# A decoder step whose GpSimd queue takes page numbers from an SBUF copy of the page table instead of DRAM

## The reference

```
page_table (DEC_BATCH, PAST_LEN // PAGE_SIZE) int32, logical page -> physical page
kidx_past = cache_kidx[page_table].reshape(b, past, IDX_DIM)
score     = sum over heads of relu(qi . kidx) * wi
_, idx    = lax.top_k(score, topk)
rows      = page_table[idx // PAGE_SIZE] * PAGE_SIZE + idx % PAGE_SIZE
k_sel, v_sel = k_pool[rows], v_pool[rows];  out = softmax(q . k_sel) @ v_sel
```

## Time and profile before

| what | value |
| --- | --- |
| median of three runs | 2094.11 us (2090.16 to 2096.39) |
| the profiled execution: span from the first to the last instruction | 2095.3 us; the page gives nothing outside it |
| PE busy | 1872.0 us, 89% |
| DVE, ACT, POOL busy | 55%, 42%, 9% |
| mean granted clock of TensorE | 0.913 of full speed |
| data moved | 365.41 MB, mean 174 GB/s |

### The profile page before, as it was taken

The page is one execution under the profiler, slowest core; times in us unless marked ns, Lnnn a source line. Parts: engine busy times, 40 slices in busy tenths (PEclk is TensorE's granted clock), DMA queues, the critical chain, the costliest instruction groups (busy, mean ns, idle before and its releaser), DMA issues.

```text
span 2095.3 us, 26096 instructions
## 1 busy us (share of the span) xinstructions
PE 1872.0 (89%) x9628; PEld 1571.3 (75%) x9628; DVE 1149.1 (55%) x1375; ACT 870.6 (42%) x987; POOL 190.7 (9%) x235
## 2 busy tenths in 40 slices
PE   6998669757998887899999989999999999997898
PEld 3998548645886666799799768867876886885798
DVE  4875335897851111122344337873885885885532
ACT  3332235445432222232132326753773773774432
POOL 1110112332321211100000000000000000000000
PEclk9999879878999887799999859997999999999999
DMA  7554213322445234347365517984995995996440
GB/s 209 133 137 115 71 51 94 88 62 79 131 142 138 89 103 132 94 127 258 123 179 144 153 41 274 366 285 145 367 366 162 364 371 188 333 366 204 141 126 26
DMA packets 389873, 365.41 MB, mean 174 GB/s; under 512 B 20804, under 2 KB 363892, under 8 KB 388664
## 3 DMA queue, kind: packets, MB, share of 16 engines
q1 hardware_dynamic: 381560, 345.03, 52.8%
q0 software_dynamic: 8192, 18.89, 3.0%
HBM read 353.15 MB, written 10.72 MB: 174 GB/s over the span
## 4 chain that ended last, share of the span: by engine, by line
PE 69%; DVE 10%; issue 9%; POOLq 9%; ACT 2%; DMA 1%; DVEq 0%; POOL 0%; SPq 0%; ACTq 0%
PE psum L1335 19%; PE psum L626 17%; POOLq L1183 8%; PE psum L643 8%; PE psum L699 5%; PE psum L1322 5%; PE psum L609 4%; PE psum L661 2%; PE psum L1263 2%; PE psum L575 1%; PE psum L692 1%; DVE arena L1980 1%; DVE arena L1978 1%; PE psum L1307 1%; ACT weights_high L1581 1%
## 5 line engine op out<-in xcount | busy, mean ns | idle before, releaser
L830 DVE TENSOR_TENSOR weights_low<-arena,weights_high 128x2048 fp32r<-128x2048 f32 x192 | 439.5, 2292 | 81.0 <-ACT weights_high L725 81.0
L1335 PE MATMUL psum<-input_high,weights_high 128*128 128x320 f32 x1264 | 414.9, 328 | 43.0 <-ACT arena L1644 23.8
L725 ACT ACTIVATE weights_high<-arena 128x2048 fp32r<-128x2048 f32 x192 | 367.3, 1916 | 90.6 <-PE psum L626 56.1
L1335 PE MATMUL psum<-input_low,weights_high 128*128 128x320 f32 x1264 | 403.8, 319 | 0.0
L1335 PE MATMUL psum<-input_high,weights_low 128*128 128x320 f32 x1264 | 403.3, 319 | 0.0
L1335 PEld LDWEIGHTS psum<-input_high,weights_high 128*128 128x128 f32 x1264 | 249.5, 197 | 59.7 <-ACT arena L1644 29.5
L1335 PEld LDWEIGHTS psum<-input_low,weights_high 128*128 128x128 f32 x1264 | 249.5, 197 | 1.2
L1335 PEld LDWEIGHTS psum<-input_high,weights_low 128*128 128x128 f32 x1264 | 248.5, 197 | 0.1
L1838 DVE TENSOR_TENSOR weights_low<-arena,weights_high 128x1024 fp32r<-128x1024 f32 x128 | 150.8, 1221 | 108.6 <-ACT weights_high L1581 108.5
L626 PE MATMUL psum<-weights_high,gathered_high 128*128 128x512 f32 x512 | 204.2, 399 | 0.0
L626 PE MATMUL psum<-weights_low,gathered_high 128*128 128x512 f32 x512 | 201.1, 393 | 0.0
(11 more groups left out here) (310 smaller groups left out, 2506.1 us busy)
## 6 DMA issues: line engine op xcount, KB each, us to landing
arena<-in_w SPq DMA_DIRECT2D x384, 512.0 KB, 7.5
arena<-in_w_in SPq DMA_DIRECT2D x64, 1024.0 KB, 5.7
arena<-in_w_out SPq DMA_DIRECT2D x16, 1024.0 KB, 5.9
arena<-in_w_ple_gate SPq DMA_DIRECT2D x16, 1024.0 KB, 6.9
arena<-in_cache_k POOLq DMA_DIRECT2D x64, 128.0 KB, 2.3
arena<-in_w_br_rnn SPq DMA_DIRECT2D x8, 1024.0 KB, 5.5
arena<-in_cache_v POOLq DMA_DIRECT2D x64, 128.0 KB, 2.3
arena<-in_w_br_attn SPq DMA_DIRECT2D x8, 1024.0 KB, 5.3
```

The costliest lines, as they stand in the source:

```text
L725: nc.scalar.activation(stage[m % STG][0][:], mslots[m % MRING], ACT.Identity).then_inc(s["high"], 1)
L830: v.tensor_tensor(lo[:], mslots[m % MRING], hi[:].bitcast(F32), ALU.subtract).then_inc(s["split"], 1)
L1335: last = mm(acc[0:m, 0:T], x[:, P * k:P * k + m], y[:], start=(k == 0 and n == 0), stop=(k == KD - 1 and n == 2))
```

## The change

The 64 table entries are copied by one DMA into a row of SBUF, `pages_i`, as POOL's first instruction. `page` then loads the register from there, and the queue waits for that copy once, ahead of the first page.

```
+        pages_i = nc.alloc_sbuf_tensor_at("pages_i", [1, NB * NPG], I32, offset=base + 4 * top[0])
+        take(NB * NPG)
...
+        pages_in = sem("pages_in")
...
         @block.gpsimd
         def _(pool):
+            pool.dma_start(pages_i[:], A["page_table"].rearrange("(o b) g -> o (b g)", o=1)).then_inc(pages_in, 16)
             nc.gpsimd.memset(wa[:], 0.0)
...
             def page(b, g):
-                return pool.value_load(A["page_table"][b:b + 1, g:g + 1], min_val=0, max_val=A["cache_k"].shape[1] - 1)
+                n = NPG * b + g
+                return pool.value_load(pages_i[0:1, n:n + 1], min_val=0, max_val=A["cache_k"].shape[1] - 1)
+
+            pool.wait_ge(pages_in, 16)
```

## The result

| | before | changed |
| --- | --- | --- |
| median (range, runs) | 2092.14 us (2084.86 to 2096.39, 4) | 1965.74 us (1964.02 to 1993.46, 4) |
| ratio, 95% interval | | 0.9435 [0.9381, 0.9488] |
| profiled execution, span | 2095.3 us | 1962.3 us (its time 1964.02) |
| mean granted clock | 0.913 | 0.952 |
| PE busy | 1872.0 us | 1815.9 us |

The change makes the kernel 126 us faster by the medians, 133.0 by the two spans. The forecast was 1981 us.

A forecast was written before the change was run, and what follows sets the result against it. POOL's issue of cache pages, not their bytes, was taken to bound index scores and sample attention. Gains of 35.9 + 79.9 = 115.8 us, less 3, gave 2095.3 - 113 = 1982, so 1981 us; range 1964 to 2020.

The forecast's parts named there:

- What bounds the kernel: Index scores and sample attention: PE waits 31.4 and 45.5 us for pages POOL issues late, then runs at low clock.
- A page's issue: POOL's queue: a page's 2.30 us falls to 1.4 with the number loaded from SBUF (1.17 to 1.42).
- The stalls: POOL's address loads of up to 3.54 us: gone if DRAM's; if the queue's, a page costs 1.65 us.
- Index scores: Both PE waits for pages of indexer keys go, with some slow clock: 35.9 us gained.
- Between the stages: From top-k to sample attention: everything shifts by the earlier gain, 0 us more, 5 us either way for DVE pieces.
- Sample attention: Six remaining passes run without waits at full clock, 173.0 us against 252.9: 79.9 us gained.
- The allowance: 3 us set against the gain because ACT and DVE get less time for the same steps.
- The sum: Whole kernel: 35.9 + 79.9 = 115.8 us, less 3; 2095.3 - 113 = 1982, so 1981.
- Low clock: Rival, sample attention: waits go but matmuls stay slow, only 77 us gained, 2017 us; chance 0.06.
- POOL binds: Rival, both stages: a page still costs 2.0 us, so some waits remain, 2018 us; chance 0.09.
- Slower: Rival, 128 pages: one SBUF load costs more than both DRAM loads; 2135 us at 2.0 us a load; chance 0.02.
- No change: Rival: PE waits at the same places for something later, such as softmax on DVE and ACT, 2094 us; chance 0.03.

The follow-up runs named there:

- e1: Changed kernel with only the indexer keys' pages numbered from SBUF, keys and values from DRAM as before; ratio 0.9797 to the kernel before, median 2058.13 us.
- e2: Changed kernel with only the keys' and values' pages numbered from SBUF, indexer keys from DRAM; ratio 0.9543 to the kernel before, median 1999.86 us.
- e6: Changed kernel without the two instructions that check a page number's bounds; ratio 0.94 to the kernel before, median 1966.27 us.
- e3: Changed kernel with each page number loaded from SBUF twice; ratio 0.9463 to the kernel before, median 1974.3 us.
- e5: Changed kernel with each page number loaded from SBUF four times; ratio 1.0098 to the kernel before, median 2116.72 us.
- e7: The changed kernel measured once more, unaltered; ratio 0.9455 to the kernel before, median 1983.97 us.
- e4: Changed kernel with each page number loaded from SBUF three times; ratio 0.9721 to the kernel before, median 2035.57 us.

## Why the prediction was right, and where its sizes were off

- **What bounds the kernel.** Right. Page issue bound both stages: e1 and e2 each win back one of them, and a third and fourth load from SBUF bring the waits back with no load of a page number from DRAM.
- **A page's issue.** The direction and the stalls were right, the price too high: I took 1.4 us, bounds 1.17 and 1.42, with 1.65 if the stalls stayed, and it is 1.15, just below them all. The load is like the quicker rows, 0.288 against 0.304 us, not like the slow single one that I chose. The error changed little: at 0.90 (e6) no more is won, and even at 1.69 (e3) the first expert group starts only 11.2 us later.
- **The stalls.** I had left open whether they were DRAM's. They come with the loads that a number in DRAM needs, in either stage: up to 4.0 us in e1 (sample attention) and 2.6 in e2 (index scores), against 1.05 in e1's loads from SBUF and 1.39 in e5's, on a queue as late as before's. What holds such a load up is not shown. The trace agrees in kind with the Trainium skill (DMA: Bandwidth & Descriptors, section "Latency and other measured facts": an HBM access takes 0.2 us on average and 2 us under high load). The measured stalls go above that second figure: 4.0 - 0.89 = 3.1 us over the median.
- **Index scores.** 35.9 us predicted; the prompt's attention behind them starts 37.5 us earlier (343.0 against 380.5). The 1.6 are not all the change's. PE reached pair 2 at 242.4 and not at 245.1: it was 1.1 us ahead at pair 0 already (206.7 against 207.8), and its clock was 1.00 from 210 to 220 us where before and e7 had 0.83. On the other side PE needs 24.4 us from pair 2 to pair 3 where I had 22.9, 1.1 of it because the wait for ACT between them grew. Such pieces differ between executions: e7 starts the prompt's attention at 340.9.
- **Between the stages.** 0 predicted, bounds of 5 us: at the second half of the first request's keys (565.6 against 605.2) 39.6 us had been won, 2.1 more than at the prompt's start. Half a us came in between; the rest is the clock behind a wait of 1.9 us that both have: 0.81 from 597 to 606 us before, 1.00 from 559 to 566 after (8.1 us from one half of the keys to the other before, 6.5 after and in e6 and e7). One piece of 5.5 us on DVE went (the longest is now 1.23), but PE still waits 30.8 us for the line that it stands in, 31.9 before.
- **Sample attention.** 79.9 us predicted, 252.9 - 173.06 = 79.8 measured. The passes that the prediction put at 28.35 us take 28.6.
- **The allowance.** 3 us set against the sum were not needed.
- **The sum.** 3 + 1.6 + 2.1 - 0.1 - 0.2 (between the last pass and the experts) = 6.4 us more than the 112.8: 119.2. To 1962.3 the 13.6 us of the expert group's clock come on top, which the prediction did not have: the profile of before holds one slow second group, that of after none. So it was partly luck that 1965.74 fell only 2 us inside the lower end of the range; e7's median, 1983.97, lies close to the forecast. The last step of the sum, from 1982 to 1981, took the 1.2 us between a span and the runs' median, though an execution's time is 1.7 us above its span (1964.02 and 1962.3).
- **The rivals.** Low clock: wrong, 1.00 stayed, but e4 shows its mechanism, with 25 us of clock for eight waits of 19 us in all. POOL binds: wrong here, right at 1.69 us a page in the index scores and from somewhere between 1.69 and 2.22 in the sample attention. The prediction's rows put these points at (268.0 - 217.1 - 2.0) / 32 = 1.53 and at 1.77; none of the runs lies between 1.15 and 1.69. Slower: its mechanism is e5's, though its premise, a dear load from SBUF, fell. No change: wrong, PE's waits for ACT from 100 to 1000 us grew by 1.1 us where 76.9 us of waits for caches went.

I found no version that is faster than the changed kernel. The waits for ACT (27.0 us from 100 to 1000 us, at two lines) and for the prompt's probabilities on DVE (30.8) that are left were not tried.

## What to carry to other kernels

A queue that only issues transfers has a price per transfer. Divide the time between two meetings of the waiting engine by the transfers in it, and compare that with the mean step, stalls included. Below that point a cheaper issue is worth nothing; above it every tenth of a us counts for all transfers, and each wait adds its piece of slow clock, here some 2 to 3 us whether it was short or long. Compare waits between two kernels over the same work and not over the same times: what moves across the edge of a window looks like a gain or a loss. And compare two profiles at a mark ahead of any stretch in which the clock varies by itself, before giving the whole difference to a change.

## What the runs showed that I had not expected

A register load from SBUF on POOL's queue takes 0.288 us, one third of the load of the table's address that it saves (0.872). A group of experts takes 167.2 or 180.8 us, at clock 1.00 or 0.92, in two executions of one program.
